# Reordering the split-weight FFN start, the norm sum and the stage-end splits of a two-block transformer kernel

## Chip, cores and metric
One NeuronCore of a Trainium2 chip runs the whole program in one launch. The metric is the device time of one execution in microseconds, the median of several runs. Engines as the profile names them: PE (TensorE), ACT (ScalarE), DVE (VectorE), POOL (GpSimd), SP (SyncE, which here only issues DMAs). "PEld" is PE's weight load.

## What is computed
256 tokens of width 1024 pass through a first block of two layers and then a second block of one layer. Each layer of the first block is FFN, attention, FFN:

```python
for layer in range(2):
    x = x + 0.5 * swiglu(rms_norm(x, norm_ffn1[layer]), w_gate, w_up, w_down)
    xn = rms_norm(x, norm_mix[layer])
    x = x + mix(xn @ w_in ...) @ w_out[layer]
    x = x + 0.5 * swiglu(rms_norm(x, norm_ffn2[layer]), w_gate2, w_up2, w_down2)
# swiglu: (silu(x @ w_gate) * (x @ w_up)) @ w_down, inner width 2816
# rms_norm: x * rsqrt(mean(x*x) + 1e-6) * g
```

`mix` is stick-breaking and block attention in layer 0, forgetting and dilated attention in layer 1. The second block (a recurrence, latent attention, a 16384-expert lookup, a gated embedding) is not touched by the change.

## The kernel before
**Split products.** In the FFNs and the QKV projections every fp32 product is made of three products in a faster format: weight and activation are each split into a high part (a rounded copy) and a low part (the rest), and `mm3` issues high·high, low·high and high·low. One weight tile of 128 x 2048 (1 MB) is loaded into a slot of a ring of six; ACT writes its high part (`high`, L1416; `high_qkv`, L1423), DVE its low part (`low`, L1815; `low_qkv`, L1820), and that subtraction frees the slot for SP's next load and tells PE that the tile is ready (`split_ready`).

**One FFN** (functions `ffn` of each engine; four of them, f = 0 to 3) works in 22 chunks c of 128 inner columns, two chunks to a group g of 11. Each group needs a gate, an up and a down tile. PE's order is: gate and up products of chunk c (24 matmuls each, 128x256 moving), then the down products of chunk c-1 (24 matmuls). For each chunk, DVE scales the two products by the norm's `rstd` (L1859), ACT applies Silu (L1478), DVE multiplies (L1862), ACT copies the high part of h (L1480), DVE makes its low part (L1864, signals `h_ready`), and behind that ACT and DVE split the weight tiles that `splits_after(c)` names: after an even chunk the down tile of the group, after an odd one gate and up of the group after next. `place(kind, g)` gives a tile's number in load and split order; SP (L641 to L666), ACT, DVE and PE all follow it. In chunk 0, up of group 1 is split first and then down of group 0. The down products of chunk 0 wait for `split_ready` of down 0 (L776) and for `h_ready` (L777).

**The norm** is not applied to x ahead of the products. The products take x times the gain, and `rstd` scales their result. ACT squares x (L1450), PE sums the squares over the partitions with 8 fp32 matmuls against ones (`norm`, L734), ACT takes Ln and Exp (L1458, L1460). In the FFN `norm(n)` stands between the gate and the up products of chunk 0 (L766). In the QKV stage (`layer`, 12 tiles s, two halves each) it stands behind the first half of tile 0 (L982); four tiny matmuls (`rcol`, L984) behind the second half turn `rstd` into a column, DVE copies it (L1972) and uses it to scale the value products on their way out of PSUM (L2000). The value products rotate through three PSUM banks, so that the fourth half waits until DVE has emptied the first.

**Around a stage's end.** In chunk 20 (`CHUNKS - 2`) ACT and DVE also split the first tiles of the next stage: QKV tile 0 after FFN 0 and 2, gate 0 and up 0 of FFN 2 after FFN 1. After chunk 21, DVE adds the four quarters of the down product to x (L1885) and makes the low parts of the next x (L1841), for which PE's next stage waits one by one.

**ACT's own DMAs.** In FFN 0, behind the norm's root, ACT issues three loads: the mask constants, a small slice of `w_in_cd` and the bias `b_f` (L1470 to L1472), and only then loads the Silu table. Each engine runs its instructions strictly in this written order.

Of the kernel before, what the change touches and what calls it, by code (L numbers as in the profile page):

```python
# [27 lines left out]
D = 1024  # L28
# [34 lines left out]
NCON = _n  # L63
# [78 lines left out]
def build(nc, A, out):  # L142
    ctx = ExitStack()
    with ctx:
# [93 lines left out]
        def splits_after(c):  # L238

            g = c // 2  # L240
            return [("down", g)] if c % 2 == 0 else [("gate", g + 2), ("up", g + 2)] if g + 2 < GROUPS else []

        def place(kind, g):

            if kind == "down":
                return 3 * g + 4 if g < GROUPS - 1 else FFN_SLOTS - 1
            return (max(3 * g - 1, 0)) + (kind == "up")
# [385 lines left out]
        def _(sp):  # L633
# [7 lines left out]
            def ffn(f):  # L641
                gate, up, down = ffn_w[f]

                def part(kind, g, i=0):

                    k = at["ffn", f] + place(kind, g)
                    n0 = i * 512 + g * 256
                    if kind == "down":
                        fetch(k, slot(k, 2, D), down[bass.ds(n0, 256), :].rearrange("(k p) n -> p k n", p=P), i)
                    else:  # L650
                        fetch(k, slot(k, KC, 256), rows(gate if kind == "gate" else up)[:, :, bass.ds(n0, 256)], i)

                def triple(g, i=0):
                    part("gate", g, i)
                    part("up", g, i)
                    part("down", g - 1, i)

                for g in range(2):
                    part("gate", g)
                    part("up", g)  # L660
                part("down", 0)
                triple(2)
                with sp.Fori(0, (GROUPS - 3) // 2) as i:
                    triple(3, i)
                    triple(4, i)
                part("down", GROUPS - 1)  # L666
# [43 lines left out]
        def _(pe):  # L710
# [33 lines left out]
            def ffn(f, n):  # L744
                base, base_s = CHUNKS * f, SPLIT0["ffn", f]

                def gate_up(c, i):
# [3 lines left out]
                    for j, kind in enumerate(("gate", "up")):  # L751
# [14 lines left out]
                        if c == 0 and j == 0:  # L766
                            norm(n)
                    ins.then_inc(gu_ready, 1)
                    if s == 1:
                        owed_pairs[0] += 1  # L770
# [188 lines left out]
            def layer(l):  # L959
# [3 lines left out]
                for s in range(QKV_SLOTS):  # L963
# [3 lines left out]
                    for half, label in enumerate(chunks_of(l, s)):  # L967
# [14 lines left out]
                        if s == 0 and half == 0:  # L982
                            norm(1 + 3 * l)
                        if s == 0 and half == 1:  # L984
# [415 lines left out]
        def _(act):  # L1400
# [61 lines left out]
            def ffn(f, n):  # L1462
# [3 lines left out]
                high(f, "gate", 1)  # L1466
                root(n)
                if f == 0:

                    act.dma_start(con[:, NFIRST:NCON], A["con"][:, NFIRST:NCON]).then_inc(S("masks_loaded"), 16)  # L1470
                    act.dma_start(WF, rows(A["w_in_cd"][0])[:, :, 3 * D : 3 * D + 8]).then_inc(S("wf_loaded"), 16)
                    act.dma_start(small[0:8, 40:41], A["b_f"].rearrange("a n -> n a")).then_inc(S("bf_loaded"), 16)  # L1472
                act.preload_act_table(ACT.Silu)

                def chunk(c, i=0):
# [5 lines left out]
                    if c == 0:  # L1481
                        high(f, "up", 1)
                    for kind, g in splits_after(c):
                        high(f, kind, g, i)
                    if c == CHUNKS - 2 and f in (0, 2):
                        high_qkv(f // 2, 0)
                    if c == CHUNKS - 2 and f == 1:
                        high(2, "gate", 0)
                        high(2, "up", 0)
# [314 lines left out]
        def _(dve):  # L1804
# [39 lines left out]
            def ffn(f, n):  # L1844
# [6 lines left out]
                low(f, "gate", 1)  # L1851
                dve.wait_ge(S("rstd_ready"), n + 1)

                def chunk(c, i=0):
# [10 lines left out]
                    if c == 0:  # L1865
                        low(f, "up", 1)
                    for kind, g in splits_after(c):
                        low(f, kind, g, i)
                    if c == CHUNKS - 2 and f in (0, 2):
                        low_qkv(f // 2, 0)  # L1870
                    if c == CHUNKS - 2 and f == 1:
# [627 lines left out]
```

## Time and profile before
| | us |
|---|---|
| median of 3 runs (2401.94 to 2405.39) | 2402.84 |
| the profiled execution, own time | 2426.5 |
| its span, first to last instruction | 2424.8 |
| PE busy (86% of the span) | 2086.9 |
| DVE busy (53%) | 1281.7 |
| ACT busy (33%) | 795.9 |

Times of the trace are microseconds from the span's start. The four FFNs lie roughly at 0 to 217, 370 to 569, 569 to 767 and 944 to 1139 us, the QKV stages start near 218 and 768. The second block runs from there to the end. An instruction's "idle before" names the engine and line whose signal ended the wait. Matmuls overlap one another, so the duration of one (0.28 us) is longer than the distance between two starts.

### The profile page before, as it was taken

To read this page: it belongs to the slowest core of one execution; us is meant where nothing else is said; L and a number is where in the kernel's file an instruction comes from. 1 tells how busy PE (TensorE), PEld (TensorE's weight loads), DVE (VectorE), ACT (ScalarE), POOL (GpSimd) and SP (SyncE) were. 2 spreads that over 40 slices of the span, in tenths; PEclk is the share of its full clock that TensorE was granted. 3 is DMA by queue.
4 is the path that set the end of the run, shared out by engine and by line. 5 is a ranking of instruction groups with operands and counts; after the bars stand their busy time and mean duration, and the time that the engine had idled before them with its cause. 6 is when DMAs were issued, how large, how long until landed. Compare 5 with 4: busy or idle time off the path is not lost.

```text
span 2424.8 us, 34935 instructions
## 1 busy us (share of the span) xinstructions
PE 2086.9 (86%) x13964; PEld 1668.9 (69%) x13964; DVE 1281.7 (53%) x2342; ACT 795.9 (33%) x1306; POOL 678.9 (28%) x702
## 2 busy tenths in 40 slices
PE   6999989998999999999994999986776776577687
PEld 6999979998999968998873887872333322232235
DVE  4555535555555634555636553275565565556422
ACT  4444344444444433444333223122211212121122
POOL 0000010000001000000007322047776777777760
PEclk9999999999999969999987998998998898789899
DMA  8554416554554404554320100579998999999990
GB/s 285 183 187 143 135 36 210 183 192 144 174 190 140 156 1 160 188 175 147 116 85 18 36 20 19 164 261 385 365 368 323 376 355 347 358 356 369 359 349 18
DMA packets 253790, 489.59 MB, mean 202 GB/s; under 512 B 13873, under 2 KB 173137, under 8 KB 253537
## 3 DMA queue, kind: packets, MB, share of 16 engines
q0 software_dynamic: 73888, 268.53, 29.5%
q1 hardware_dynamic: 176016, 214.32, 27.2%
q10 hardware_dynamic: 3760, 5.02, 0.7%
q8 instruction: 85, 1.39, 0.2%
q14 instruction: 41, 0.33, 0.0%
HBM read 486.74 MB, written 1.05 MB: 201 GB/s over the span
## 4 chain that ended last, share of the span: by engine, by line
PE 68%; POOL 10%; DVE 7%; issue 6%; DMA 4%; ACT 3%; another core or an unknown queue 1%; ACTq 0%; DVEq 0%; POOLq 0%
PE bank L715 67%; POOL arena_sb L2457 8%; POOL con_sb L2457 2%; DMA con_sb<-peer_v,arena_sb 2%; DVE parts_sb L1815 1%; DMA arena_sb<-peer_u,arena_sb 1%; DMA arena_sb<-peer_v,arena_sb 1%; ACT parts_sb L1416 1%; PE bank L866 1%; DVE arena_sb L2127 0%; DVE xn_sb L1828 0%; DVE parts_sb L1834 0%; DVE xT_sb L1885 0%; DVE xl_sb L1841 0%
## 5 line engine op out<-in xcount | busy, mean ns | idle before, releaser
L715 PE MATMUL bank<-arena_sb 64*64 64x64 f32 (+8 forms) x3704 | 544.3, 333 | 180.6 <-ACT arena_sb L1762 81.8
L715 PE MATMUL bank<-xh_sb,parts_sb 128*128 128x256 f32 x3328 | 603.5, 284 | 17.0 <-DVE parts_sb L1815 16.4
L715 PEld LDWEIGHTS bank<-arena_sb 64*64 64x64 f32 (+4 forms) x3704 | 320.7, 168 | 398.2 <-issue 285.6
L715 PEld LDWEIGHTS bank<-xh_sb,parts_sb 128*128 128x128 f32 x3328 | 512.8, 189 | 23.4 <-issue 22.1
L715 PE MATMUL bank<-xl_sb,parts_sb 128*128 128x256 f32 x1808 | 508.9, 281 | 0.0
L2338 DVE CUSTOM_DVE_ANT_0 sq_sb<-arena_sb 128x1024 f32<-128x1024 f32 x256 | 309.1, 1224 | 263.1 <-DMA arena_sb<-peer_u,arena_sb 230.5
L1815 DVE TENSOR_TENSOR parts_sb<-ring_sb,parts_sb 128x2048 fp32r<-128x2048 f32 x132 | 298.5, 2290 | 180.3 <-ACT parts_sb L1416 180.3
L715 PEld LDWEIGHTS bank<-xl_sb,parts_sb 128*128 128x128 f32 x1808 | 342.5, 189 | 0.0
L2457 POOL DMA_INDIRECT arena_sb<-peer_u,arena_sb x256 | 275.8, 1077 | 193.9 <-DVE arena_sb L2308 110.1
L715 PE MATMUL bank<-h_high_sb,parts_sb 128*128 128x256 f32 x1408 | 264.2, 288 | 18.4 <-DVE parts_sb L1815 14.7
L1416 ACT ACTIVATE parts_sb<-ring_sb 128x2048 fp32r<-128x2048 f32 x132 | 247.9, 1910 | 64.5 <-PE bank L715 63.6
L715 PEld LDWEIGHTS bank<-h_high_sb,parts_sb 128*128 128x128 f32 x1408 | 224.6, 196 | 19.8 <-DVE parts_sb L1815 15.6
L715 PE MATMUL bank<-con_sb,arena_sb 128*128 128x512 f32 (+1 forms) x512 | 189.3, 519 | 50.0 <-DMA con_sb<-peer_v,arena_sb 45.7
L1762 ACT ACTIVATE arena_sb<-con_sb,arena_sb 128x128 f32<-128x128 f32 x256 | 89.2, 394 | 349.5 <-PE bank L715 163.8
L715 PE MATMUL bank<-h_low_sb,parts_sb 128*128 128x256 f32 x704 | 202.0, 287 | 0.0
L2457 POOL DMA_INDIRECT arena_sb<-peer_v,arena_sb x160 | 180.5, 1128 | 68.8 <-issue 44.6
L715 PEld LDWEIGHTS bank<-con_sb,arena_sb 128*128 128x128 f32 (+1 forms) x512 | 74.7, 178 | 160.3 <-issue 157.3
L715 PE MATMUL bank<-xn_sb,ring_sb 128*128 128x256 f32 (+1 forms) x656 | 148.6, 385 | 3.4 <-DVE xn_sb L1828 3.2
L715 PEld LDWEIGHTS bank<-xn_sb,ring_sb 128*128 128x128 f32 (+1 forms) x656 | 123.4, 190 | 26.9 <-issue 9.0
L715 PEld LDWEIGHTS bank<-h_low_sb,parts_sb 128*128 128x128 f32 x704 | 138.0, 196 | 0.0
L715 PE MATMUL bank<-arena_sb,ring_sb 128*128 128x256 f32 (+2 forms) x592 | 134.1, 390 | 2.6 <-issue 2.6
L715 PEld LDWEIGHTS bank<-arena_sb,ring_sb 128*128 128x128 f32 (+2 forms) x592 | 114.1, 193 | 23.2 <-issue 5.0
(261 smaller groups left out, 1910.4 us busy)
## 6 DMA issues: line engine op xcount, KB each, us to landing
ring_sb<-ffn_w_gate SPq DMA_DIRECT2D x44, 1024.0 KB, 5.4
ring_sb<-ffn_w_up SPq DMA_DIRECT2D x44, 1024.0 KB, 6.7
ring_sb<-ffn_w_down SPq DMA_DIRECT2D x44, 1024.0 KB, 4.9
ring_sb<-w_in SPq DMA_DIRECT2D x17, 1024.0 KB, 5.3
ring_sb<-w_in_ab SPq DMA_DIRECT2D x12, 1024.0 KB, 5.0
ring_sb<-w_out SPq DMA_DIRECT2D x12, 1024.0 KB, 4.9
ring_sb<-w_in_cd SPq DMA_DIRECT2D x12, 1024.0 KB, 6.2
ring_sb<-peer_w_q SPq DMA_DIRECT2D x8, 1024.0 KB, 5.3
```

The lines of the kernel that those rows point to most:

```text
L715: return pe.matmul(dst, lhsT, rhs, start=start, stop=stop_, skip_group_check=loose)
L866: ins = pe.transpose(b[:, dst : dst + P], pr[:, src : src + P], ident)
L1416: act.activation(whi(f, kind, g), ring[:, k % RING, :], ACT.Copy).then_inc(hi_ready, 1)
L1762: act.activation(DG[n % ND], ident, ACT.Copy, scale=WT[:, tb, 16 * h + e : 16 * h + e + 1]).then_inc(S("diag_ready"), 1)
L1815: dve.tensor_tensor(wlo(f, kind, g), ring[:, k % RING, :], whi(f, kind, g), ALU.subtract).then_inc(split_ready, 1)
L2338: dve.tensor_tensor_reduce(JUNK[n % 2], UROW[n % NU], HTOK[:, tb, :], 1.0, 0.0, ALU.mult, ALU.add, DOTS[:, tb, 16 * h + e : 16 * h + e + 1 ...
L2457: pool.indirect_dma_start(out=row[n % len(row)], out_offset=None, in_=A[table][0], in_offset=bass.IndirectOffsetOnAxis(ap=EIDX[:, tb, 16 * ...
```

## The change
Five orders are altered; the arithmetic is the same.
- In `ffn`, down 0 takes place 3 and up 1 place 4 of the load and split order; ACT and DVE split down 0 ahead of the norm's root, and only up 1 after chunk 0 (it comes from `splits_after(0)`).
- PE's `norm(n)` stands behind all of chunk 0's gate and up products.
- In the QKV stage `norm` stands behind the second half of tile 0, and the `rcol` matmuls behind the first half of tile 1.
- ACT's three DMA issues of FFN 0 stand behind chunk 2's split of down 1.
- The next stage's low parts are made in chunk 21 in place of chunk 20; the high parts too for up 0 of FFN 2.

(The change's title also has the squares on ACT; they are there before it as well.)

```diff
--- before.py
+++ after.py
@@ -238,10 +238,14 @@
         def splits_after(c):
 
             g = c // 2
+            if c == 0:
+                return [("up", 1)]
             return [("down", g)] if c % 2 == 0 else [("gate", g + 2), ("up", g + 2)] if g + 2 < GROUPS else []
 
         def place(kind, g):
 
+            if (kind, g) in (("down", 0), ("up", 1)):
+                return 3 if kind == "down" else 4
             if kind == "down":
                 return 3 * g + 4 if g < GROUPS - 1 else FFN_SLOTS - 1
             return (max(3 * g - 1, 0)) + (kind == "up")
@@ -655,10 +659,11 @@
                     part("up", g, i)
                     part("down", g - 1, i)
 
-                for g in range(2):
-                    part("gate", g)
-                    part("up", g)
+                part("gate", 0)
+                part("up", 0)
+                part("gate", 1)
                 part("down", 0)
+                part("up", 1)
                 triple(2)
                 with sp.Fori(0, (GROUPS - 3) // 2) as i:
                     triple(3, i)
@@ -763,9 +768,9 @@
                                 release(first)
                         if s == 1 and j == 0:
                             ins.then_inc(pair_used, 1)
-                        if c == 0 and j == 0:
-                            norm(n)
                     ins.then_inc(gu_ready, 1)
+                    if c == 0:
+                        norm(n)
                     if s == 1:
                         owed_pairs[0] += 1
 
@@ -979,9 +984,9 @@
                             if kk == 0:
                                 release(head_)
                         fill_end(ins, label)
-                        if s == 0 and half == 0:
+                        if s == 0 and half == 1:
                             norm(1 + 3 * l)
-                        if s == 0 and half == 1:
+                        if s == 1 and half == 0:
                             b = fill_begin(pe, ("rcol", l))
                             pe.wait_ge(S("rstd_ready"), 2 + 3 * l)
                             for tb in range(2):
@@ -1464,12 +1469,8 @@
                 if f == 0:
                     high(f, "up", 0)
                 high(f, "gate", 1)
+                high(f, "down", 0)
                 root(n)
-                if f == 0:
-
-                    act.dma_start(con[:, NFIRST:NCON], A["con"][:, NFIRST:NCON]).then_inc(S("masks_loaded"), 16)
-                    act.dma_start(WF, rows(A["w_in_cd"][0])[:, :, 3 * D : 3 * D + 8]).then_inc(S("wf_loaded"), 16)
-                    act.dma_start(small[0:8, 40:41], A["b_f"].rearrange("a n -> n a")).then_inc(S("bf_loaded"), 16)
                 act.preload_act_table(ACT.Silu)
 
                 def chunk(c, i=0):
@@ -1478,14 +1479,17 @@
                     act.activation(gate, gate, ACT.Silu).then_inc(silu_ready, 1)
                     act.wait_ge(hraw_ready, base + c + 1 + 4 * i)
                     act.activation(HH[:, c % 2, :], h, ACT.Copy).then_inc(hh_ready, 1)
-                    if c == 0:
-                        high(f, "up", 1)
                     for kind, g in splits_after(c):
                         high(f, kind, g, i)
+                    if c == 2 and f == 0:
+                        act.dma_start(con[:, NFIRST:NCON], A["con"][:, NFIRST:NCON]).then_inc(S("masks_loaded"), 16)
+                        act.dma_start(WF, rows(A["w_in_cd"][0])[:, :, 3 * D : 3 * D + 8]).then_inc(S("wf_loaded"), 16)
+                        act.dma_start(small[0:8, 40:41], A["b_f"].rearrange("a n -> n a")).then_inc(S("bf_loaded"), 16)
                     if c == CHUNKS - 2 and f in (0, 2):
                         high_qkv(f // 2, 0)
                     if c == CHUNKS - 2 and f == 1:
                         high(2, "gate", 0)
+                    if c == CHUNKS - 1 and f == 1:
                         high(2, "up", 0)
 
                 for c in range(3):
@@ -1849,6 +1853,7 @@
                     low(0, "gate", 0)
                     low(0, "up", 0)
                 low(f, "gate", 1)
+                low(f, "down", 0)
                 dve.wait_ge(S("rstd_ready"), n + 1)
 
                 def chunk(c, i=0):
@@ -1862,13 +1867,11 @@
                     dve.tensor_tensor(h, gate, h, ALU.mult).then_inc(hraw_ready, 1)
                     dve.wait_ge(hh_ready, base + c + 1 + 4 * i)
                     dve.tensor_tensor(HL[:, c % 2, :], h, HH[:, c % 2, :], ALU.subtract).then_inc(h_ready, 1)
-                    if c == 0:
-                        low(f, "up", 1)
                     for kind, g in splits_after(c):
                         low(f, kind, g, i)
-                    if c == CHUNKS - 2 and f in (0, 2):
+                    if c == CHUNKS - 1 and f in (0, 2):
                         low_qkv(f // 2, 0)
-                    if c == CHUNKS - 2 and f == 1:
+                    if c == CHUNKS - 1 and f == 1:
                         low(2, "gate", 0)
                         low(2, "up", 0)
```

## Rows read from the trace of the kernel before
**Rows 1.** The page, part 4: the chain that ended last, by engine.
```profile
PE 68%; POOL 10%; DVE 7%; issue 6%; DMA 4%; ACT 3%; another core or an unknown queue 1%; ACTq 0%; DVEq 0%; POOLq 0%
```

**Rows 2.** Waits of PE, 0 to 1170 us: us in total, times, longest.
```profile
PE bank L715 <- DVE parts_sb L1815: 31.1, 5, 16.4
```

**Rows 3.** Windows: busy us (x count) by engine, PE clock, DMA share, GB/s.
```profile
32.95:39.09 6.14, 0.00 (x1) 0.01 (x1) 4.76 (x4) 3.35 (x2) 0.00 (x0) 0.82 1.12 337
...
39.09:44.06 4.97, 4.97 (x24) 4.97 (x25) 2.62 (x4) 3.90 (x4) 0.00 (x0) 0.54 1.07 377
...
384.99:387.86 2.87, 0.00 (x1) 0.01 (x1) 2.87 (x3) 0.09 (x1) 0.00 (x0) 1.00 0.33 75
...
387.86:392.32 4.46, 4.46 (x24) 4.46 (x25) 2.12 (x4) 3.39 (x4) 0.00 (x0) 0.62 1.06 394
...
563.42:566.09 2.67, 0.00 (x0) 0.00 (x0) 1.65 (x4) 1.32 (x3) 0.00 (x0) 0.96 1.06 343
...
203.79:212.34 8.55, 8.55 (x74) 8.55 (x73) 5.21 (x5) 4.57 (x4) 0.00 (x0) 1.00 0.03 4
```

**Rows 4.** Timeline, start of the second FFN: start us, us, engine, instruction, idle before.
```profile
372.86 3.62 PE L715 MATMUL bank<-arena_sb,con_sb 128*128 128x256 f32 x16
...
373.69 1.89 ACT L1416 ACTIVATE parts_sb<-ring_sb 128x2048 fp32r<-128x2048 f32 x1
...
376.51 0.47 ACT L1458 ACTIVATE std_sb<-bank,con_sb 128x256 f32<-128x256 f32 x1 [0.93 <-PE bank L715]
...
377.45 1.28 ACT L1473 ACT_TABLE_LOAD   x1
...
379.40 0.69 DVE L1859 TENSOR_TENSOR sgate_sb<-bank,rstd_sb 128x512 f32<-128x512 f32 x1 [1.49 <-PE bank L715]
...
383.31 4.50 DVE L1815 TENSOR_TENSOR parts_sb<-ring_sb,parts_sb 128x2048 fp32r<-128x2048 f32 x2 [1.38 <-ACT parts_sb L1416]
...
387.72 0.68 DVE L1859 TENSOR_TENSOR hT_sb<-bank,rstd_sb 128x512 f32<-128x512 f32 x1
```

**Rows 5.** Start of the first FFN on ScalarE; one DMA issue row (KB, us to landing).
```profile
18.09 1.91 ACT L1416 ACTIVATE parts_sb<-ring_sb 128x2048 fp32r<-128x2048 f32 x1 [0.24 <-DMA ring_sb<-ffn_w_gate]
...
25.84 4.21 ACTq L1472 DMA_DIRECT2D small_sb<-b_f  x1
...
con_sb<-con ACTq DMA_DIRECT2D x1, 1657.0 KB, 11.5
```

**Rows 6.** VectorE timeline, ends of the first and (last two rows) second FFN.
```profile
208.67 2.29 DVE L1815 TENSOR_TENSOR parts_sb<-ring_sb,parts_sb 128x2048 fp32r<-128x2048 f32 x1 [2.37 <-ACT parts_sb L1416]
...
210.88 2.29 DVE L1820 TENSOR_TENSOR parts_sb<-ring_sb,parts_sb 128x2048 fp32r<-128x2048 f32 x1
...
213.08 0.68 DVE L1859 TENSOR_TENSOR hT_sb<-bank,rstd_sb 128x512 f32<-128x512 f32 x1
...
215.16 0.42 DVE L1864 TENSOR_TENSOR h_low_sb<-hT_sb,h_high_sb 128x256 fp32r<-128x256 f32 x1 [0.48 <-ACT h_high_sb L1480]
...
216.65 1.41 DVE L1885 SCALAR_TENSOR_TENSOR xT_sb<-bank,xT_sb 128x512 f32<-128x512 f32 x2 [1.07 <-PE bank L715]
...
556.93 6.70 DVE L1815 TENSOR_TENSOR parts_sb<-ring_sb,parts_sb 128x2048 fp32r<-128x2048 f32 x3 [2.37 <-ACT parts_sb L1416]
...
572.45 1.66 DVE L1841 SCALAR_TENSOR_TENSOR xl_sb<-xT_sb,vec_sb,xh_sb 128x256 fp32r<-128x256 f32 x4
```

**Rows 7.** Timeline, start of the first QKV stage; last row: the chain in order.
```profile
227.20 2.29 DVE L1820 TENSOR_TENSOR parts_sb<-ring_sb,parts_sb 128x2048 fp32r<-128x2048 f32 x1 [4.78 <-ACT parts_sb L1423]
...
229.28 0.60 PE L715 MATMUL bank<-con_sb,rstd_sb 1*128 1x1 f32 x4
...
229.99 0.16 DVE L1972 COPY small_sb<-bank 128x2 f32<-128x2 f32 x1 [0.50 <-PE bank L715]
...
230.19 0.89 DVE L2000 TENSOR_SCALAR arena_sb<-bank,small_sb 128x256 f32<-128x256 f32 x2
...
221.29 77.92 PE bank L715 x600
```

## Prediction
> **What bounds the kernel now.** I read the chain of waits first: PE holds 68% of it [rows 1], and up to 1140 us, where all edits lie, it is nearly all PE. So an edit counts only if it moves PE. Then PE's waits there: one pair stands out, PE waiting for DVE's weight subtraction, 31.1 us in 5 waits [rows 2]. The longest of them, 16.4 us, is the program's first load and stays. The other four are one in each FFN, all ahead of the down products of chunk 0. The windows show them: nothing on PE from 32.95 to 39.09 in the first FFN, and from 384.99 to 387.86 in the second [rows 3]; the third and fourth repeat that second pattern (at 586.76 and 958.57). A fifth hole of 2.67 us stands ahead of the last down products of FFN 1 (563.42). Behind each hole the 24 down products are slow: the granted clock is 0.54 to 0.63, between the two levels (1.2 and 2.4 GHz), and they take 4.97 and 4.46 us [rows 3]. An undisturbed stretch holds 72 matmuls in 8.55 us, so 24 take 2.85 us [rows 3].
>
> **Down 0 ahead of up 1, in the four FFNs.** Before, ACT and DVE turn to the two tiles only after chunk 0's h (the pair of subtractions begins at 383.31 and takes 4.50), and down 0 is the second: PE resumes at 387.86 [rows 3, 4]. After: ACT's high of gate 1 runs 373.69 to 375.6, high of down 0 to 377.5; DVE's low of gate 1 to 377.9, of down 0 to 380.2 (1.89 for a copy [rows 4], 2.29 for a subtraction [rows 6]). PE wants it at 384.9. So this wait goes, if h is in time.
>
> **Is h in time?** The norm's sum is now behind the up products. They are 24 matmuls, 2.85 us. The sum started at 372.86 and Ln at 376.51, 3.65 later [rows 4]; now it starts at 375.7, Ln at 379.35, rstd at 380.3, Silu table (1.28) to 381.6. DVE scales at 380.3, Silu starts at 381.6, and multiply, high and low of h follow at about 0.45 each: h ready at 383.4. PE wants it at 384.9, its own order holding the same matmuls as before. Slack 1.5 us, and this is what is late next. Price of no cover: one for one, and the slow clock again if the hole nears 2.7 us. The copy of down 0 (1.9) lies in ACT's wait for the sum.
> DVE then makes low of up 1 until 387.1, so chunk 1's scale starts 387.1 (before 387.72), while PE is 2.2 us further on. Chunk 1's splits end some 8.3 us after its scale: to the pair's end it is 379.40 to 387.8, 8.4, in chunk 0 [rows 4], and chunk 1 has the same steps; chunk 2's scale is at 395.4 against 393.75 when PE offers it; its down tile is then done 6.2 us later, at 401.6, wanted at 402.05. That is the tightest place, 0.45 us.
>
> **Gain of the four starts.** The idle counts run from the end of a matmul of 0.28, whereas matmuls start 0.119 apart, so a hole costs 0.16 more than its idle. Second FFN: 2.87 + 0.16 + (4.46 - 2.85) = 4.64. Third and fourth alike, together 13.9. First: 6.14 + 0.16 + (4.97 - 2.85) = 8.4. There the 3.27 us excess of the hole comes from ACT's DMA issues: the one at 25.84 took 4.21 [rows 5] and the table load stood behind it. After, the table is loaded at 28.3 to 29.6, h ready at about 31.3, PE wants it at 32.8; down 0 is the fourth load, 3 us behind gate 1's (landed 18.09 [rows 5]), split by 25.3. Sum 22.3.
>
> **The three DMA issues moved.** They hold ACT 5.1 us (estimated from the 4.21 of the last and under 0.5 for each other) behind chunk 2's copy, at 47.2 to 52.3. Queued behind them is chunk 3's Silu, due 50.7: 1.6 late. PE needs that h only 8.5 us after its gate and up; nothing on PE. The later split after chunk 4 has 0.8 left. Bounds: 0 to the full 5.1; I take 0. SP's ring loads share the engines with the 1657 KB [rows 5] in either place. The Trainium skill (DMA: Bandwidth & Descriptors, Rules for kernel authors) speaks against this part: it says to issue a DMA early and wait for it late. Here the wait is at the QKV stage past 217 us and con landed 11.5 us after issue, so the rule costs nothing in this place; by it the sum would be the same.
>
> **Low parts behind chunk 21.** At the ends of FFN 0 and 2, DVE's QKV subtraction (210.88 to 213.17) delayed the last chunk's scale to 213.08; 8.55 after the one before it would be 212.34. h was ready 2.5 us after the scale, and PE resumed at 215.63 [rows 6]: now PE has no gap (saves 0.47). But the residual adds, which began at 216.65 [rows 6], now stand behind the subtraction: 212.34 + 2.5 + 2.2 = 217.0. From there the chain of adds and low parts of x is DVE's own, so PE's QKV start is 0.4 later: a loss.
> At the end of FFN 1 three subtractions (556.93, 6.70 [rows 6]) gave the 2.67 hole. Now the last scale is at 560.6, h at 563.1, no hole; down products end 566.3. DVE does both subtractions 563.0 to 567.45 and then adds. With the chain's 5.8 us (in the first FFN from 216.65 to 222.4; an estimate from 4 adds of 0.6 to 0.7 and 8 low parts of 0.4), the last low of x is at 573.2, against 574.1 before [rows 6]: gain 0.9. PE is now idle 566.3 to 569.2, 2.9 us, as long as the holes that were followed by the low clock [rows 3].
> The Trainium skill (TensorE: Matmul & The Clock Gate, What's actually happening) has it that throttled is the default and activity releases it; the trace agrees, since the clock fell behind 2.67 us. [...]
> My own bound from rows: the products behind it are paced by DVE anyway, so a low clock costs 0 to 1.6 (a 4.46 in place of 2.85). I take 0.4, as most of the slow stretch lies under that pacing. Net gain here 0.5.
>
> **QKV stage, twice.** Before: `rcol` at 229.28, DVE's copy 229.99, value products drained from 230.19, the first of the two by 230.65 (half of 0.89) [rows 7]; PE meanwhile had the first half of tile 1 (2.8 us) to run. After, the order is half, half, sum, half, rcol, half. The sum ends at 229.5; tile 1's low part ended 229.49 and is 0.4 later, 229.9, so PE waits 0.4 (which contains the late start). Half to 232.7, rcol at 232.8, drained 1.4 later, 234.2; the next half wants the bank of the first and waits from 233.35: 0.9. Before, tile 1 ended at 235.4; after, 237.05. Loss 1.6, twice 3.3. Bounds: 0 (if a later wait had room; but the chain stays on PE for 77.9 us from 221.29 [rows 7], so none has) to 2 x 2.5. I take 3.3.
>
> **Sum.** 22.3 + 0.5 - 3.3 = 19.5 us off the profiled execution's 2426.5. The profiled one is 1% longer than the median; I take the same microseconds off the median: 2402.84 - 19.5 = 2383.3.
>
> **Rivals.**
> (A) The wait changes its name: h of chunk 0 (through sum, Ln, Exp, table, Silu) is late in place of the split. For: the slack of 1.5 us is small and made of eight hand-overs. Against: each of their times is in rows 4. If each of the four starts keeps a 1.5 us hole, without the clock's fall: + 6, 2389; if 2 us and the slow clock (1.6) stay: 4 x 3.6 = 14.4, 2398.
> (B) The QKV reorder is free, because DVE's and ACT's splits have slack behind it and the 3.3 is made up before the stage ends: 2380. Against: PE is without gaps there, so it sets the pace.
> (C) Slower. DVE enters the loop 2.2 us later against PE than before. If the down split of the even chunks does not catch up (0.45 us at 402 is the place), each group waits: from a lateness of over 0.45 that persists, 1.0 us a group in 9 groups of 4 FFNs is 36 us: 2419. Against: an even chunk's chain ends 7.2 us after its scale (203.79 to 210.96 [rows 3, 6]), 6.2 when its release is not waited for, of 8.55; it regains over 1 us each time.
>
> **Numbers.** Forecast as written 0.64, A 0.18, B 0.14, C 0.04. The likeliest case alone spans 2379 to 2388; with most of A and B, 2378 to 2392. About 0.2% (4.8 us) is what a measurement of this kernel tells from no change. Faster takes the forecast, B and nearly all of A: 0.94; the end of A beyond 2398 gives 0.03 same; C 0.03 slower.
>
> **What would show it.** No idle on PE ahead of the down products of chunk 0, in four places, and a clock of 1.0 there; PE's first window to 215 us shorter by 8 to 9 us; each of FFN 1, 2, 3 by 4.6; a new PE wait of 0.9 behind `rcol` and 0.4 ahead of QKV tile 1; PE idle near 2.9 us between FFN 1 and 2. I am wrong if PE waits for L1864 there (A), if waits for L1815 recur in the loop (C), or if QKV is no longer than before (B).

## Result and the profile after

| | before | after |
|---|---|---|
| median, us | 2404.11 (2397.75 to 2414.88, 6 runs) | 2384.82 (2380.47 to 2390.64, 6 runs) |
| profiled execution, us | 2426.5 | 2380.47 |

The ratio is 0.9906, 95% interval 0.9878 to 0.9934: 19.3 us faster, where 19.5 were forecast. In time the interval is 16 to 29 us, so it is luck that the two numbers agree to 0.2 us; the terms below are what tests the working. The two profiled executions differ by 46 us, and 29 of these lie in the second block, which the change does not touch. So the traces are read up to the first product of the second block, and the rest is taken up below.

The page of the changed kernel (span; busy by engine; chain by engine): PE's busy time is what it was, its share rose because idle time went.

```profile
span 2378.7 us, 34935 instructions
...
PE 2085.0 (88%) x13964; PEld 1671.7 (70%) x13964; DVE 1280.7 (54%) x2342; ACT 797.5 (34%) x1306; POOL 671.8 (28%) x702
...
PE 70%; POOL 11%; DVE 6%; DMA 5%; issue 5%; ACT 3%; DVEq 0%; ACTq 0%
```

PE's waits up to 1170 us (total, times, longest), against [rows 2]. Of the five waits for the weight subtraction (L1819 now) only the program's first is left. The waits for the low parts of x have grown (2.1 us in 6 waits before, 0.4 at most), and those for the value products' drain (L2003), two of them, are new.

```profile
PE bank L720 <- DVE parts_sb L1819: 16.3, 1, 16.3
...
PE bank L720 <- DVE xl_sb L1845: 6.5, 8, 3.0
...
PE bank L720 <- DVE arena_sb L2003: 1.7, 2, 0.8
```

The changed kernel in windows (columns as in [rows 3]). The 24 down products of chunk 0 now take 2.86 and 2.87 us at full clock in FFN 0 and 1, where [rows 3] have 4.97 and 4.46. The first row is the first 4 us of PE's work: 19 matmuls, 0.21 us from start to start where full pace has 0.12. (The clock column says 1.00 there; the pace speaks against it.) In the last two rows, between FFN 1 and 2, PE is idle half of 6 us, and the 48 gate and up products behind take 7.90 us at a mean clock of 0.78, part of them at the 1.2 GHz level.

```profile
16.30:20.30 4.00, 4.00 (x19) 4.00 (x20) 2.52 (x2) 3.37 (x2) 0.00 (x0) 1.00 1.05 386
...
33.80:36.66 2.86, 2.86 (x26) 2.86 (x25) 2.81 (x2) 0.01 (x1) 0.00 (x0) 1.00 1.10 347
...
380.38:383.25 2.87, 2.87 (x27) 2.87 (x25) 2.82 (x2) 0.02 (x1) 0.00 (x0) 1.00 0.58 192
...
554.20:560.24 6.04, 3.02 (x26) 2.85 (x25) 6.04 (x6) 3.63 (x5) 0.00 (x0) 1.00 0.57 171
...
560.24:568.14 7.90, 7.55 (x48) 7.31 (x49) 4.62 (x10) 7.06 (x12) 0.00 (x0) 0.78 0.43 160
```

Start of the second FFN, ACT and then DVE, against [rows 4]: both high parts ahead of the norm's Ln (369.25, x2), h's low part at 378.50, chunk 2's scale at 390.81 and the down tile split behind it at 394.70.

```profile
369.25 3.70 ACT L1421 ACTIVATE parts_sb<-ring_sb 128x2048 fp32r<-128x2048 f32 x2
...
374.90 0.47 ACT L1463 ACTIVATE std_sb<-bank,con_sb 128x256 f32<-128x256 f32 x1 [1.95 <-PE bank L720]
...
375.84 1.28 ACT L1474 ACT_TABLE_LOAD   x1
...
375.86 0.69 DVE L1864 TENSOR_TENSOR sgate_sb<-bank,rstd_sb 128x512 f32<-128x512 f32 x1 [0.18 <-ACT rstd_sb L1465]
...
378.50 0.42 DVE L1869 TENSOR_TENSOR h_low_sb<-sgate_sb,h_high_sb 128x256 fp32r<-128x256 f32 x1 [0.48 <-ACT h_high_sb L1481]
...
390.81 0.68 DVE L1864 TENSOR_TENSOR sgate_sb<-bank,rstd_sb 128x512 f32<-128x512 f32 x1
...
394.70 2.29 DVE L1819 TENSOR_TENSOR parts_sb<-ring_sb,parts_sb 128x2048 fp32r<-128x2048 f32 x1 [1.39 <-ACT parts_sb L1421]
```

Start of the first FFN on ACT, against [rows 5]: down 0's high part; the last DMA issue, 2.50 us where it took 4.21; chunk 3's Silu.

```profile
20.54 1.91 ACT L1421 ACTIVATE parts_sb<-ring_sb 128x2048 fp32r<-128x2048 f32 x1 [0.65 <-DMA ring_sb<-ffn_w_down]
...
46.79 2.50 ACTq L1487 DMA_DIRECT2D small_sb<-b_f  x1
...
51.92 0.42 ACT L1479 ACTIVATE hT_sb<-hT_sb 128x256 f32<-128x256 f32 x1 [3.84 <-DVE hT_sb L1864]
```

The ends of the first (three rows) and second FFN (two rows) on DVE, against [rows 6]: the last chunk's scale now waits for PE alone, and the subtraction stands behind it and ahead of the adds.

```profile
204.93 0.69 DVE L1864 TENSOR_TENSOR hT_sb<-bank,rstd_sb 128x512 f32<-128x512 f32 x1 [1.38 <-PE bank L720]
...
207.36 2.28 DVE L1824 TENSOR_TENSOR parts_sb<-ring_sb,parts_sb 128x2048 fp32r<-128x2048 f32 x1
...
209.56 1.28 DVE L1888 SCALAR_TENSOR_TENSOR xT_sb<-bank,xT_sb 128x512 f32<-128x512 f32 x2
...
553.95 4.49 DVE L1819 TENSOR_TENSOR parts_sb<-ring_sb,parts_sb 128x2048 fp32r<-128x2048 f32 x2
...
562.40 1.66 DVE L1845 SCALAR_TENSOR_TENSOR xl_sb<-xT_sb,vec_sb,xh_sb 128x256 fp32r<-128x256 f32 x4
```

Start of the first QKV stage, against [rows 7]: tile 1 waits 0.19 for its low part, and the half behind `rcol` waits 0.84 for the drain.

```profile
222.40 0.38 PE L720 MATMUL bank<-parts_sb,xh_sb 128*128 128x256 f32 x1 [0.19 <-DVE parts_sb L1824]
...
225.39 0.60 PE L720 MATMUL bank<-con_sb,rstd_sb 1*128 1x1 f32 x4
...
226.83 0.38 PE L720 MATMUL bank<-parts_sb,xh_sb 128*128 128x256 f32 x1 [0.84 <-DVE arena_sb L2003]
...
226.09 0.16 DVE L1975 COPY small_sb<-bank 128x2 f32<-128x2 f32 x1 [3.75 <-PE bank L720]
```

**Where the time went.** The starts of the same matmul in both traces, before minus after, give a running gain:

| point (before, after) | gain | step |
|---|---|---|
| FFN 0, down of chunk 20 (212.13, 204.73) | 7.40 | +7.4 |
| QKV 0, tile 1's second half (232.62, 226.83) | 5.79 | -1.6 |
| FFN 1, first gate product (369.68, 365.23) | 4.45 | -1.35 |
| FFN 1, down of chunk 20 (560.39, 551.32) | 9.07 | +4.62 |
| FFN 2, gate of chunk 1 (580.74, 571.41) | 9.33 | +0.26 |
| FFN 2, down of chunk 20 (762.15, 748.22) | 13.93 | +4.60 |
| FFN 3, first gate product (943.24, 931.19) | 12.05 | -1.9 |
| FFN 3, down of chunk 20 (1133.96, 1117.27) | 16.69 | +4.64 |

(The points 232.62 and 580.74 are worked out: 229.81 and 577.89 with 24 matmuls added to each.) The prediction's terms at these places were +8.4, -1.6, none, +4.64, +0.5, +4.64, -1.6 and +4.64.

### The profile page after: what moved, and what is told of

Same layout as the page of the kernel before. It is cut to its first block, busy times and chain, and to the rows that moved or that the text cites. A ratio compares the mean times of both kernels' runs of the same rounds, so it can differ in the third digit from the quotient of the medians.

```text
span 2378.7 us, 34935 instructions
## 1 busy us (share of the span) xinstructions
PE 2085.0 (88%) x13964; PEld 1671.7 (70%) x13964; DVE 1280.7 (54%) x2342; ACT 797.5 (34%) x1306; POOL 671.8 (28%) x702
## 4 chain that ended last, share of the span: by engine, by line
PE 70%; POOL 11%; DVE 6%; DMA 5%; issue 5%; ACT 3%; DVEq 0%; ACTq 0%
PE bank L720 69%; POOL arena_sb L2460 8%; DMA arena_sb<-peer_u,arena_sb 3%; POOL con_sb L2460 2%; DMA con_sb<-peer_v,arena_sb 1%; PE bank L871 1%; DVE parts_sb L1824 0%; DVE xT_sb L1888 0%; DVE arena_sb L2130 0%; DVE xn_sb L1832 0%; DVE parts_sb L1838 0%; DVE parts_sb L1819 0%; DMA arena_sb<-peer_v,arena_sb 0%; DVE sq_sb L2341 0%; DMA xT_sb<-xT 0%
## 5 line engine op out<-in xcount | busy, mean ns | idle before, releaser
L720 PE MATMUL bank<-arena_sb 64*64 64x64 f32 (+8 forms) x3704 | 554.4, 339 | 159.9 <-ACT arena_sb L1766 126.2
L720 PEld LDWEIGHTS bank<-arena_sb 64*64 64x64 f32 (+4 forms) x3704 | 330.3, 171 | 376.4 <-issue 213.7
L1819 DVE TENSOR_TENSOR parts_sb<-ring_sb,parts_sb 128x2048 fp32r<-128x2048 f32 x132 | 298.7, 2290 | 174.9 <-ACT parts_sb L1421 174.9
L2460 POOL DMA_INDIRECT arena_sb<-peer_u,arena_sb x256 | 284.5, 1111 | 193.3 <-DVE arena_sb L2311 109.4
L720 PE MATMUL bank<-h_high_sb,parts_sb 128*128 128x256 f32 x1408 | 255.8, 282 | 0.0
L720 PEld LDWEIGHTS bank<-h_high_sb,parts_sb 128*128 128x128 f32 x1408 | 218.2, 191 | 0.0
L2460 POOL DMA_INDIRECT arena_sb<-peer_v,arena_sb x160 | 169.7, 1060 | 51.2 <-issue 42.0
```

The costliest lines, as they stand in the source:

```text
L720: return pe.matmul(dst, lhsT, rhs, start=start, stop=stop_, skip_group_check=loose)
L1819: dve.tensor_tensor(wlo(f, kind, g), ring[:, k % RING, :], whi(f, kind, g), ALU.subtract).then_inc(split_ready, 1)
L2460: pool.indirect_dma_start(out=row[n % len(row)], out_offset=None, in_=A[table][0], in_offset=bass.IndirectOffsetOnAxis(ap=EIDX[:, tb, 16 * ...
```

## Experiments

Most kernels leave the second block out and store x after the fourth FFN (labels with t_). They take 1.12 to 1.15 ms and spread over 2 to 5 us, so that single parts of the change can be read. Line numbers in them are lower by about 20 to 40. The first four of the table ran on one chip, the next four on a second, the last two and the two whole programs at the end on a third. The changed kernel was not run on the second, so the medians of t_nonorm to t_best are held against another chip's; on the first and third, t_after differs by 0.6 us.

| kernel | median, us (runs, lowest to highest) |
|---|---|
| t_before | 1145.84 (4, 1144.14 to 1148.28) |
| t_after | 1127.23 (4, 1126.08 to 1128.39) |
| t_split | 1124.52 (4, 1123.34 to 1125.28) |
| t_noqkv | 1128.67 (4, 1123.77 to 1129.17) |
| t_nonorm | 1125.82 (4, 1125.08 to 1128.17) |
| t_nolow | 1129.34 (4, 1127.46 to 1131.33) |
| t_nodma | 1129.88 (4, 1128.41 to 1131.47) |
| t_best | 1122.37 (4, 1120.12 to 1124.86) |
| t_after_again | 1127.79 (5, 1125.95 to 1128.04) |
| t_noqkv_again | 1127.97 (5, 1123.99 to 1128.35) |

### The first block alone, before and after


> The kernel before, with the second block left out (x is stored after the fourth FFN); it is the base for the other shortened kernels. From the trace of before, whose fourth FFN ends at 1140.6 us, all theories expect about 1146 us, with the same five holes on PE as in the full kernel (6.1, 2.9, 2.7, 2.9, 2.9 us) and a spread between runs far under the 17 us of the full kernel if that spread comes from the second block.

> The changed kernel, second block left out. My theory: 19.5 us under the shortened kernel before by the sum of the prediction, 16.7 by the shift of the last common point of the two profiles (1149.02 to 1132.34). Rival (the gain lies in the second block, where the two profiles differ by another 29 us): under 10 us.

18.6 us apart: the timed gain lies in the first block, and the rival falls. The spread fell from 17 us to 4, as expected if the second block makes it. In the profiled pair FFN 3's down of chunk 20 starts 20.24 us earlier (1137.17, 1116.93). Of these, 3.4 are a slower clock of t_before's run in layer 1's attention: from `rcol` to FFN 3's first down products it takes 185.47 us, the whole kernel before 182.08 with the same instructions. Without them 16.8 are left, as in the first pair. The waits of PE in t_before (its L1775 is L1815):

```profile
PE bank L694 <- DVE parts_sb L1775: 29.8, 5, 15.8
```

### One part alone: down 0 ahead of up 1
```diff
 # before, with the new place(), splits_after(), SP's load order, and
+                high(f, "down", 0)        # ACT, ahead of root(n)
+                low(f, "down", 0)         # DVE, ahead of the wait for rstd
```


> Shortened; before with one part of the change alone: down 0 loaded and split ahead of up 1 in the four FFNs. My theory: this part is nearly the whole gain. FFN 1 to 3 gain 4.64 each (13.9); in FFN 0 h is ready at 33.2, as before, and PE wants it at 32.8, so 0.4 of the hole of 6.3 stays and 8.0 goes: 21.9 us under the shortened kernel before, and so 2.4 faster than all parts together. Rival 1 (the split needs the later norm sum to pay): 10 or less. Rival 2 (all parts add up): slower than the shortened changed kernel.

21.3 us under t_before (21.9 expected), 2.7 faster than the whole change, and no run of one overlaps with a run of the other. So this part is the whole gain, and the other parts together cost. The traces give the same sum: t_after is 0.7 ahead behind FFN 0, and loses 1.65 and 1.56 in the two QKV and attention stages and 0.93 at the end of FFN 1.

Of the waits that this is about, two remain besides the first load. A wait of 0.4 us was expected ahead of chunk 0's down products, for h. It is not there: PE waits 0.46 us ahead of chunk 2's, for the down tile (third row): the place that the prediction called the tightest, and its rival C, of which this is a mild case. The slip costs 0.7 us in FFN 0 and ends there; the chunks behind have the usual 8.55 us. The 2.7 us hole at the end of FFN 1 is the second wait. Here no low clock follows it, and the products behind it take 2.97 us (last row), where t_before has 4.45. So a hole of this length is not always followed by the low clock.

```profile
PE bank L699 <- DVE parts_sb L1779: 16.5, 2, 16.1
...
PE bank L699 <- DVE h_low_sb L1829: 3.6, 3, 2.7
...
51.22 0.51 PE L699 MATMUL bank<-h_high_sb,parts_sb 128*128 128x256 f32 x2 [0.46 <-DVE parts_sb L1779]
...
553.15:555.83 2.68, 0.00 (x2) 0.00 (x1) 1.66 (x4) 1.33 (x3) 0.00 (x0) 1.00 1.07 344
...
555.83:558.80 2.97, 2.97 (x25) 2.96 (x25) 1.93 (x4) 2.01 (x5) 0.00 (x0) 1.00 1.05 391
```

### QKV order back
```diff
-                        if s == 0 and half == 1:
+                        if s == 0 and half == 0:
                             norm(1 + 3 * l)
-                        if s == 1 and half == 0:
+                        if s == 0 and half == 1:
...
```


> Shortened; the changed kernel with the norm sum and rcol of the QKV stage at their old places. My theory: 1.2 us a layer come back (the wait of 0.84 behind rcol and 0.4 ahead of tile 1 go): 2.5 us faster than the shortened changed kernel, and no PE wait for DVE L2003. Rival (DVE and ACT make up for it later in the stage): the same within 0.3 us.

> The shortened kernel with the old QKV order again. Its median came out 1.4 above the shortened changed kernel, though its QKV stages were 1.2 shorter each in the trace: three of its four runs had a clock of 0.968 to 0.970. My theory: run against run at the same clock it is 2.3 faster (1123.8 at 0.974), and its slower runs are those with a longer low clock in layer 1's attention. Rival (the old order itself costs time): no run of it is faster than the fastest of the other.

> The shortened changed kernel again, for its spread and granted clock: my theory is that runs with mean clock 0.974 lie near 1126.2 and those with 0.973 near 1128.2, since what differs between runs is how long the low clock holds in layer 1's attention and at the first matmuls, not an order of work.

The medians put it 1.4 and 0.2 us above t_after; read by them the expectation failed. The stage itself did shorten: from FFN 0's down of chunk 20 to FFN 1's first down products t_after has 175.67 us (204.45 to 380.12), t_noqkv 174.30 (203.49 to 377.79), 1.4 less. What takes it back is the granted clock in layer 1's attention. Windows over it, t_after and then t_noqkv:

```profile
840.00:940.00 100.00, 94.50 (x481) 76.00 (x480) 34.57 (x113) 35.66 (x72) 2.18 (x4) 0.78 0.18 58
```

```profile
840.00:940.00 100.00, 94.92 (x462) 77.82 (x461) 32.14 (x111) 33.71 (x68) 2.18 (x4) 0.73 0.17 54
```

0.78 against 0.73, and from layer 1's `rcol` to FFN 3's first down products t_noqkv takes 183.98 us (762.97 to 946.95) where t_after takes 177.49 (768.51 to 946.00); 1.9 of the 6.5 us is work that stands on the other side of `rcol` (one half of 2.8, less the wait of 0.9), so 4.6 is the clock's. By runs: the two of the nine of t_noqkv with a mean clock of 0.974 took 1123.77 and 1123.99, the four of t_after with 0.974 took 1125.95 to 1126.41. That is 2.2 us faster at the same clock, as forecast. The other seven had 0.968 to 0.970 and took 1127.47 to 1129.17; all nine of t_after had 0.973 or 0.974. The forecast for t_after_again held (1125.95 and 1125.98 at 0.974, 1127.79 to 1128.04 at 0.973). So the rival falls by its own test. That it is mere chance is unlikely, since what differs is how often the slower case comes; but it is not the QKV order alone either. t_split has the old order and 0.973 or 0.974 in all four runs, t_nolow below has the new one and 0.968 to 0.970 in three of four. Why, no run settles.

### The FFN's norm sum back between gate and up
```diff
+                        if c == 0 and j == 0:
+                            norm(n)
                     ins.then_inc(gu_ready, 1)
-                    if c == 0:
-                        norm(n)
```


> Shortened; the changed kernel with the FFN's norm sum back between gate and up of chunk 0. My theory: PE has the same matmuls either way and h of chunk 0 has 1.5 us of slack in the changed order, so the time is the same within 0.3 us, while rstd comes 2.9 us earlier and h of chunk 0 is ready 1.8 us earlier. Rival (the later sum is what takes the holes away): holes come back at chunk 0, 4 x 2 us or more slower.

1.4 us below t_after's median, on another chip, with the same clocks (0.3 was expected; the ranges overlap); its profiled run (1128.17) equals t_after's slower ones, and no hole came back. h's low part in FFN 1 starts at 377.55, where t_after has it at 378.24 with its down products 0.16 earlier (380.12 against 380.28). So it is 0.85 earlier and not 1.8, since the scale now waits behind down 0's subtraction:

```profile
377.55 0.42 DVE L1829 TENSOR_TENSOR h_low_sb<-sgate_sb,h_high_sb 128x256 fp32r<-128x256 f32 x1 [0.48 <-ACT h_high_sb L1450]
```

### Low parts back in chunk 20
```diff
-                    if c == CHUNKS - 1 and f == 1:
+                    if c == CHUNKS - 2 and f == 1:
                         high(2, "up", 0)      # ACT
...
-                    if c == CHUNKS - 1 and f in (0, 2):
+                    if c == CHUNKS - 2 and f in (0, 2):
                         low_qkv(f // 2, 0)    # DVE
-                    if c == CHUNKS - 1 and f == 1:
+                    if c == CHUNKS - 2 and f == 1:
                         low(2, "gate", 0)
                         low(2, "up", 0)
```


> Shortened; the changed kernel with the next stage's low parts (and high of up 0 of FFN 2) back in chunk 20. My theory: the ends of FFN 0 and 2 get 0.3 faster each, the end of FFN 1 loses 0.3 to 1.0 (the hole of 2.7 ahead of the last down products is back, the hole of 3.0 behind them goes): between 0.6 faster and 0.4 slower than the shortened changed kernel. Rival (this part is worth its place): 2 us or more slower.

The hole of 2.7 us is back, within this row of PE's waits:

```profile
PE bank L699 <- DVE h_low_sb L1829: 3.6, 3, 2.7
```

From FFN 1's down of chunk 20 to FFN 2's first down products it takes 25.21 us, t_after 25.90: against this version the change loses 0.7 us there. The last low part of x is no earlier in t_after (12.74 us behind the down of chunk 20, 12.71 here; 13.72 in the kernel before). The 0.7 is the low clock behind the hole of 3.0. It lies on the gate products: at half pace they fall behind DVE's low parts, and the up products start 1.20 us behind the last low part (563.80, 565.00) instead of 0.50 (561.51, 562.01). The 24 up products take the same time in both:

```profile
562.14 1.66 DVE L1805 SCALAR_TENSOR_TENSOR xl_sb<-xT_sb,vec_sb,xh_sb 128x256 fp32r<-128x256 f32 x4
...
565.00:567.84 2.84, 2.84 (x27) 2.84 (x25) 0.75 (x1) 2.84 (x3) 0.00 (x0) 1.00 0.02 6
```

```profile
559.85 1.66 DVE L1805 SCALAR_TENSOR_TENSOR xl_sb<-xT_sb,vec_sb,xh_sb 128x256 fp32r<-128x256 f32 x4
...
562.01:564.86 2.85, 2.85 (x26) 2.85 (x25) 0.06 (x1) 2.85 (x4) 0.00 (x0) 1.00 0.02 6
```

(First t_after, then t_nolow. All 48 take 7.87 us there and 6.08 here, but 1.1 of that difference is only that here PE comes to them later, when more low parts are ready.) At the end of FFN 0 it costs 0.2 (20.66 us from the down of chunk 20 to `rcol` in t_after, 20.44 here). The median is nevertheless 2.1 above t_after's: three of its four runs have a clock of 0.968 to 0.970, and layer 1's attention is at 0.73 as in t_noqkv. The one at 0.973 took 1127.46, t_after's at 0.973 1127.79 to 1128.39. So by the medians the rival holds (2 us or more slower), and by that one run and the stretches above my theory does.

### DMA issues back
```diff
                 root(n)
+                if f == 0:
+                    act.dma_start(con[:, NFIRST:NCON], ...)
+                    act.dma_start(WF, ...)
+                    act.dma_start(small[0:8, 40:41], ...)
                 act.preload_act_table(ACT.Silu)
```


> Shortened; the changed kernel with ACT's three DMA issues back ahead of the Silu table load. My theory: with the norm sum late, the issues (some 5 us) stand wholly on h of chunk 0 of FFN 0: PE waits there 2.5 to 3.6 us, with the low clock behind it 4 to 5.5 us slower than the shortened changed kernel. Rival (the issues are hidden behind PE's chunk 1): the same.

2.6 us slower by the medians. PE waits 1.79 us for h's low part, and from there to the last down FFN 0 takes 171.93 us against 170.94. No low clock follows this hole. The 1.0 is mostly a second wait: DVE is late by h, PE waits 0.64 us for chunk 2's down tile (second row), and the chunks behind have 8.65 and then 8.55 us again. In all 3.0 (1.8 + 0.16 + 1.0), less than the 4 to 5.5 expected: the last issue took 2.80 us and not 4.21, and the low clock stayed away. (The two profiled executions end only 0.35 us apart, as t_nodma's was 1.3 us faster in the first 48 products and 1.35 in layer 0's attention, where its clock was 0.967 and t_after's 0.956.)

```profile
34.06 0.48 PE L699 MATMUL bank<-h_high_sb,parts_sb 128*128 128x256 f32 x2 [1.79 <-DVE h_low_sb L1829]
...
52.04 0.50 PE L699 MATMUL bank<-h_high_sb,parts_sb 128*128 128x256 f32 x2 [0.64 <-DVE parts_sb L1779]
...
28.01 2.80 ACTq L1446 DMA_DIRECT2D small_sb<-b_f  x1
```

### A version without the parts that cost
```diff
 # the changed kernel with the QKV order, the FFN's norm sum and low_qkv at their old places, and
                     if c == CHUNKS - 1 and f == 1:
                         low(2, "gate", 0)
-                        low(2, "up", 0)
...
+                if f == 1:                # behind the last low_x
+                    low(2, "up", 0)
```


> Shortened; the changed kernel with the QKV order, the FFN's norm sum and the low part of QKV tile 0 back at their old places, and the low part of FFN 2's up 0 behind the residual adds. My theory: 2.5 (QKV) + 0.6 (ends of FFN 0 and 2) + 2.9 (the hole of 3.0 us between FFN 1 and 2 shrinks to 0.8 and the clock stays up) = 6.0 us faster than the shortened changed kernel. Rival for the last part: up 0's low part is then late for PE and the wait only moves: 3 us faster.

4.9 us under t_after (6.0 expected), by medians of two chips and with t_best's runs in two pairs: 1120.12 and 1120.33 at a clock of 0.976, 1124.41 and 1124.86 at 0.971. In the profiled runs (t_best's is 1120.33) the lead is 7.7: 0.8 in the program's first products, 1.7 and 2.3 in the QKV and attention stages, 2.9 at the end of FFN 1. The adds start at 553.39, up 0's low part stands behind them at 559.03, PE waits 0.82 in place of 3.02, and the stretch from FFN 1's down of chunk 20 to FFN 2's first down products is 23.03 us, 2.9 less than t_after:

```profile
555.29 0.48 PE L699 MATMUL bank<-xh_sb,parts_sb 128*128 128x256 f32 x2 [0.82 <-DVE xl_sb L1805]
...
553.39 1.28 DVE L1847 SCALAR_TENSOR_TENSOR xT_sb<-bank,xT_sb 128x512 f32<-128x512 f32 x2
...
559.03 2.28 DVE L1779 TENSOR_TENSOR parts_sb<-ring_sb,parts_sb 128x2048 fp32r<-128x2048 f32 x1
```

> The whole program with down 0 ahead of up 1, ACT's DMA issues behind chunk 2, low parts for FFN 2 behind chunk 21 (gate 0) and behind the residual adds (up 0), and the norm sums, rcol and the low part of QKV tile 0 at their old places. My theory: 4 to 6 us under the changed kernel's median on the same chip, as the shortened ones differ by 4.9; 23 to 26 under before. Rival (the second block's own changes of 10 to 20 us from run to run hide it): no order between this and the changed kernel.

> The changed kernel unaltered, timed on the same chip as the one before it. My theory: 18 to 20 us under before (the shortened pair differs by 18.6), whatever the median of before is on this chip (2404, 2409 and 2424 us so far). Rival (the 46 us of the first pair of profiles are real): 30 or more.

On the whole program the two are level: 2402.25 us (2393.88 to 2408.70), ratio 0.9884 (0.9848 to 0.9921), and 2402.29 us (2399.77 to 2410.80), ratio 0.9891 (0.9858 to 0.9925), against 2429.94 for before on this chip. The rival was right: no order between them. The profiled pair shows both reasons. In layer 1's attention the changed kernel had a clock of 0.80 and the other 0.73,

```profile
840.00:940.00 100.00, 94.51 (x504) 77.47 (x503) 35.97 (x114) 36.44 (x73) 2.28 (x4) 0.80 0.22 73
```

```profile
840.00:940.00 100.00, 94.91 (x476) 80.19 (x473) 35.43 (x114) 37.16 (x74) 2.28 (x4) 0.73 0.22 73
```

so that both reach FFN 3's down of chunk 20 at the same time (1113.00 and 1113.13 us). From there to the end they take 1286.4 and 1284.9 us; the first profile of the same changed kernel took 1261.4 (2378.7 - 1117.27), the kernel before 1290.8. So 25 us of the 29 that the first pair of profiles differ by in the second block are within what one kernel does from run to run, and the 46 us of that pair are not the change's. They lie in the expert lookup: from the first to the last of its 512 row gathers (POOL's DMAs) it is 730.5 us in the first profile of the changed kernel, 750.8 in its second, 749.5 in best_full's and 760.7 before; the rest of the way from FFN 3's down of chunk 20 to the end takes 530.0 to 535.6 in all four. The changed kernel is 27.7 under before here where I expected 18 to 20; its interval (18 to 35 us) just holds that.

## Why the prediction was right, step by step

**Down 0 ahead of up 1: right.** Three starts forecast at 4.64 each gave 4.62, 4.60 and 4.64. The working also holds inside. The second FFN starts 4.45 us earlier than before; h was forecast for 383.4, so 378.95, and came at 378.93; chunk 2's scale for 395.4, so 390.95, and came at 390.81; the down tile behind it for 401.6, so 397.15, and was done at 396.99. The tightest place held, and rival C (a lateness that persists in the loop) falls: no wait for L1819 recurs. How tight it is, t_split and t_nodma show: there PE waits 0.46 and 0.64 at this very place, once each, and the loop regains it as the prediction argued. Rival A (h late) falls too; t_nodma shows what it costs when it is true. That this part alone makes the gain is shown by t_split.

**The first FFN: mechanism right, 1.0 too much.** The hole and the slow products behind it went (8.4), but gate and up of chunk 0, the program's first 48, took 8.36 us (16.30 to 24.66) where they took 4.43 and 2.86 before: the pace rose from 0.21 to 0.12 us a matmul 5.9 us behind the first one, and 3.5 before. This is not the order's doing as far as the runs tell: with the same order the 48 took 8.43 in t_after_again, 7.19 in t_noqkv and 7.25 in the second profile of the changed kernel (15.93 to 23.18).

**The three DMA issues: right that nothing on PE waits.** Chunk 3's Silu started 0.03 us behind DVE's scale, at 51.92: no delay at all. The issues began at 45.94 and not at 47.2, the Silu was wanted 1.2 later than forecast (PE's slow start), and the last issue ended at 49.29; with 4.21 it would have ended at 51.00, still in time. What I did not weigh: with the norm sum moved and the issues left, they would have cost 3.0. By t_split, which leaves both alone and loses 0.7 in FFN 0, the move by itself is worth little; it mends what the later sum would break.

**Low parts in chunk 21: right in its steps, wrong in one price.** At the ends of FFN 0 and 2 the adds came 0.3 later, as worked out. At the end of FFN 1 the last low part of x was forecast at 573.2, less 9.07: 564.13; it ended at 564.06. The term of the sum that was mis-sized is the low clock behind the hole: I took 0.4 of at most 1.6, saying that DVE paces the products behind it. That was the right mechanism, but at half pace PE cannot keep up with DVE, and it cost 0.7: the up products start 1.25 us behind the last low part (564.06, 565.31) and not 0.5. They themselves run at full clock; the low stretch is the first row, on the gate products:

```profile
561.45:564.86 3.41, 3.32 (x15) 3.29 (x16) 2.61 (x7) 2.93 (x7) 0.00 (x0) 0.50 0.59 231
...
565.31:568.14 2.83, 2.83 (x26) 2.83 (x25) 0.79 (x1) 2.83 (x3) 0.00 (x0) 1.00 0.03 6
```

So the net against the kernel before is 0.98 - 0.72 = +0.26 in the profiled pair, where +0.5 was forecast. Against t_nolow it is -0.7: there the old order, in a run where the low clock sets in 1.3 us after PE resumes and not at once, has the last low part as early. What the old order is worth thus depends on where the low clock falls; in t_split it did not fall at all, and that stretch took 24.97 us, 0.93 less than in t_after.

**QKV order: right,** 1.6 forecast, 1.6 and 1.5 measured. Rival B (it is made up later in the stage) falls.

**What no step had:** 1.35 and 0.4 us given back in the two attention stages, where no instruction changed. The first is the granted clock: the second profile of the same changed kernel takes 153.64 us from `rcol` to FFN 1's first down products at a mean clock of 0.967, where the first took 154.99 at 0.956:

```profile
225.39:380.38 154.99, 143.13 (x990) 129.62 (x989) 77.39 (x136) 65.17 (x100) 9.27 (x32) 0.96 0.38 123
```

```profile
223.91:377.55 153.64, 141.83 (x989) 128.30 (x989) 77.34 (x136) 65.19 (x100) 9.33 (x32) 0.97 0.37 124
```

The 0.4 in layer 1 is of the size that the clock moves there (177.52 and 176.07 us in the same two profiles), but no run sets it apart.

The sum to the second block was 16.7 us in the profiled pair and 18.6 in the timed shortened pair, for 19.5 forecast. The 2.8 that the profiled pair lacks are the late clock at the start (1.0), the attention stages (1.7) and the low clock behind the hole (0.3), less 0.2 that the QKV order cost under its price. In the medians of the whole program they are less than what the second block changes by from run to run.

## What to carry to other kernels

Where two pieces are prepared by a slow helper, prepare them in the order in which the bound engine wants them; here that alone was worth 21.3 us, more than all five parts of the change together (18.6). A reordering that fills no hole on the bound engine can still open one (the QKV order and the low parts did), so each part wants its own run. When a profiled pair differs by twice what the timed runs do, cut the program to the part that changed, and compare runs at the same granted clock.

## What was not expected of the hardware

In layer 1's attention PE is busy 94 to 95% of 840 to 940 us, in a mix of small products, transposes and waits, and the granted clock is 1.2 GHz for 37 to 55 us on end; the mean over that window was 0.80, 0.78 or 0.73 in the traces shown, and runs of one kernel differ by up to 5 us with it. In t_noqkv the longest stretch came in 7 of 9 runs, judged by the mean clock, in t_after in 0 of 9; the two kernels differ in the order of a few matmuls near 225 and 770 us.

The hole of 2.7 us at the end of FFN 1 was followed by the low clock in the kernel before, in t_before and in t_nolow, and not in t_split. The holes of 2.9 and 3.0 us were followed by it in every trace that has them, the one of 1.8 in t_nodma and those of 0.8 were not.

The issue of the tiny load of `b_f` on ACT's queue, right behind a load made of 32-byte pieces, held ACT 4.21, 3.54, 3.44 and 2.80 us in the four traces where it stands behind the norm's root, and 1.23 to 2.61 in the ten where it stands behind chunk 2. What sets it within either group, no run shows.

The same kernel before had medians of 2404, 2409, 2424 and 2430 us in four sessions, on at least three chips. Its first block was run alone in one of them only (1144.14 to 1148.28 us). The four profiles of whole programs put their difference in the second block into the stretch of the expert gathers (730.5 to 760.7 us); what makes a gather stretch long is open.
